# Gated feed-forward tiles: the rounded copies go from VectorE to ScalarE, one group later

## The reference, cut to what matters

```python
def conv_glu(h, w_up, conv_w, conv_b, w_down):
    seq = h.shape[1]
    up = h @ w_up
    up_pad = jnp.pad(up, ((0, 0), (CONV_WIDTH - 1, 0), (0, 0)))
    c = conv_b
    for j in range(CONV_WIDTH):
        c = c + conv_w[j] * up_pad[:, j:j + seq]
    gate, val = _split(c, (D_FF, D_FF))
    return (jax.nn.silu(gate) * val) @ w_down
```

## Time and profile before

| | us |
|---|---|
| median of 3 runs | 2054.72 |
| lowest, highest | 2047.13, 2056.26 |
| the profiled execution | 2048.42 |
| its span in the trace | 2046.5 |

### The profile page before, as it was taken

How to read it: one execution, slowest core, us unless ns; L and a number is a source line. 1 busy time by engine, 2 the same in 40 slices (tenths; PEclk the granted TensorE clock), 3 DMA queues, 4 the chain that set the end, 5 groups by cost and what they waited for, 6 DMA issues and landing times.

```text
span 2046.5 us, 44566 instructions
## 1 busy us (share of the span) xinstructions
PE 1883.6 (92%) x16390; PEld 1778.9 (87%) x16390; DVE 1293.0 (63%) x1943; ACT 1140.5 (56%) x1924; POOL 1037.9 (51%) x742
## 2 busy tenths in 40 slices
PE   8889889999999889888999999988899998879999
PEld 8778779999999778778999989866899997669999
DVE  3487725669913397824669963476786536777764
ACT  5653455456755654445557755665555457465544
POOL 5663449839986573448929985741200045411000
PEclk9999989999999999979999999997999999779999
DMA  6432015656665432005656664420366653205665
GB/s 208 122 103 71 23 39 158 176 145 186 188 187 164 124 114 74 23 22 154 176 151 179 187 173 133 150 89 21 112 183 202 193 166 113 72 17 154 186 193 173
DMA packets 146922, 271.20 MB, mean 133 GB/s; under 512 B 16433, under 2 KB 16946, under 8 KB 146738
## 3 DMA queue, kind: packets, MB, share of 16 engines
q1 hardware_dynamic: 145296, 264.97, 45.2%
q10 hardware_dynamic: 1442, 3.66, 0.5%
HBM read 267.52 MB, written 1.05 MB: 131 GB/s over the span
## 4 chain that ended last, share of the span: by engine, by line
PE 65%; DVE 15%; ACT 9%; POOL 8%; issue 3%; DMA 0%; ACTq 0%; DVEq 0%; SPq 0%
PE bank L649 63%; POOL ring_split L1317 8%; ACT arena L1351 7%; ACT hi_ring L1351 1%; PE bank L758 1%; DVE arena L1891 1%; DVE u L1961 1%; DVE arena L1890 1%; DVE arena L2062 1%; DVE arena L1975 1%; DVE arena L1974 0%; DVE arena L2109 0%; DVE arena L1973 0%; ACT L1351 0%; DVE arena L2464 0%
## 5 line engine op out<-in xcount | busy, mean ns | idle before, releaser
L1317 POOL TENSOR_TENSOR ring_split<-ring,hi_ring 128x512 fp32r<-128x512 f32 x682 | 969.1, 1449 | 736.7 <-ACT hi_ring L1351 730.9
L1351 ACT ACTIVATE hi_ring<-ring 128x512 fp32r<-128x512 f32 x1002 | 619.3, 630 | 555.1 <-PE bank L649 532.0
L649 PE MATMUL bank<-u_hi,hi_ring 128*128 128x256 f32 (+1 forms) x2480 | 676.1, 285 | 47.3 <-POOL ring_split L1317 39.7
L649 PE MATMUL bank<-u_split,hi_ring 128*128 128x256 f32 (+1 forms) x2480 | 665.4, 281 | 1.6 <-DVE u_split L1966 1.4
L649 PE MATMUL bank<-u_hi,ring_split 128*128 128x256 f32 (+1 forms) x2480 | 665.0, 281 | 0.0
L649 PEld LDWEIGHTS bank<-u_hi,hi_ring 128*128 128x128 f32 (+1 forms) x2480 | 452.3, 188 | 61.8 <-POOL ring_split L1317 41.1
L649 PEld LDWEIGHTS bank<-u_split,hi_ring 128*128 128x128 f32 (+1 forms) x2480 | 452.4, 188 | 4.0 <-DVE u_split L1966 2.4
L649 PEld LDWEIGHTS bank<-u_hi,ring_split 128*128 128x128 f32 (+1 forms) x2480 | 452.2, 188 | 0.9
L1999 DVE TENSOR_TENSOR ring_split<-ring,hi_ring 128x512 fp32r<-128x512 f32 x320 | 215.3, 694 | 111.9 <-ACT hi_ring L1351 108.1
L649 PE MATMUL bank<-arena 64*64 64x64 f32 (+6 forms) x3680 | 240.3, 255 | 14.6 <-DVE arena L2109 9.3
L649 PEld LDWEIGHTS bank<-arena 64*64 64x64 f32 (+3 forms) x3680 | 210.4, 155 | 49.5 <-issue 29.7
(11 more groups left out here) (246 smaller groups left out, 2407.0 us busy)
## 6 DMA issues: line engine op xcount, KB each, us to landing
ring<-in_stream SPq DMA_DIRECT2D x1002, 256.0 KB, 2.8
par<-in_params ACTq DMA_DIRECT2D x3, 637.0 KB, 4.3
h<-in_x SPq DMA_DIRECT2D x4, 256.0 KB, 4.3
cst<-in_cst SPq DMA_DIRECT2D x1, 993.0 KB
out<-h ACTq DMA_DIRECT2D x3, 256.0 KB, 2.8
par<-in_params ACTq DMA_DIRECT2D x1, 633.0 KB, 8.3
out<-h ACTq DMA_DIRECT2D x2, 128.0 KB, 2.3
msk<-in_masks SPq DMA_DIRECT2D x1, 104.0 KB
```

The lines of the kernel that those rows point to most:

```text
L649: ins = nc.tensor.matmul(o, l, r, start=start, stop=stop)
L1317: G.tensor_tensor(ring_lo[:, c, :], ring[:, c, :], hi_ring[:, q % HI_RING, :].bitcast(F32), ALU.subtract).then_inc(lo_by_pool, 1)
L1351: return nc.scalar.activation(o, i, f, **kw)
```

## The change

In the U loop of the first kind, VectorE no longer makes the rounded copy `hidden_hi`. ScalarE makes it, one turn later: in turn i it copies tile i - 2, behind its Silu of tile i - 1, once VectorE has signalled the product (new signal `hidden_in`). VectorE subtracts in the same turn, once ScalarE has signalled the copy (new signal `hidden_high`). Both loops have one turn more. ScalarE's wait before it reuses a `cb` buffer is now for the product instead of the low part. Three weight roundings that stood behind the table load now stand in the loop: one behind the last eviction, one ahead of the last Silu, one behind it.

```diff
@@ scalar, the U loop
-                for i in range(23):
+                for i in range(24):
                     if i < 22:
                         hi.upto(f"U{i}")
                         bank = B.wait(act, f"U{i}")
                         if i >= 4:
-                            act.wait_ge(S["hidden_ready"], past["hidden_ready"] + i - 3)
+                            act.wait_ge(S["hidden_in"], past["hidden_in"] + i - 3)
...
                         act.sem_inc(S["conv_in"], 1)
-                    if i:
+                    if i in (21, 22):
+                        hi.more()
+                    if 0 < i < 23:
                         act.wait_ge(S["conv_mid"], past["conv_mid"] + i)
                         C.link(A(cb[(i - 1) % 4][:, 0, :], cb[(i - 1) % 4][:, 0, :], ACT.Silu), S["conv_out"])
+                    if i == 22:
+                        hi.more()
+                    if i > 1:
+                        act.wait_ge(S["hidden_in"], past["hidden_in"] + i - 1)
+                        C.link(A(hidden_hi[:, i - 2, :], hidden[:, i - 2, :], ACT.Copy), S["hidden_high"])
                 nc.scalar.preload_act_table_set(LN_EXP)
@@ vector, the U loop
-                for i in range(23):
+                for i in range(24):
...
-                    if i:
+                    if 0 < i < 23:
                         dve.wait_ge(S["conv_out"], past["conv_out"] + i)
                         c_ = cb[(i - 1) % 4]
-                        C.link(V.tensor_tensor(hidden[:, i - 1, :], c_[:, 0, :], c_[:, 1, :], ALU.mult))
-                        split(C, hidden[:, i - 1, :], hidden_hi[:, i - 1, :], hidden_lo[:, i - 1, :], S["hidden_ready"])
+                        C.link(V.tensor_tensor(hidden[:, i - 1, :], c_[:, 0, :], c_[:, 1, :], ALU.mult), S["hidden_in"])
+                    if i > 1:
+                        dve.wait_ge(S["hidden_high"], past["hidden_high"] + i - 1)
+                        C.link(V.tensor_tensor(hidden_lo[:, i - 2, :], hidden[:, i - 2, :], hidden_hi[:, i - 2, :].bitcast(F32), ALU.subtract), S["hidden_ready"])
```

More of the change, by code:

```diff
@@ L410 @@
     "conv_in": (0, 22, 22, 20), "conv_mid": (0, 22, 22, 4), "conv_out": (0, 22, 22, 4),
-    "hidden_ready": (0, 22, 22, 16), "h_ready": (0, 10, 10, 10), "fresh_norm": (0, 1, 1, 0), "bi_ready": (0, 2, 2, 0),
+    "hidden_ready": (0, 22, 22, 16), "hidden_in": (0, 22, 22, 0), "hidden_high": (0, 22, 22, 0), "h_ready": (0, 10, 10, 10), "fresh_norm": (0, 1, 1, 0), "bi_ready": (0, 2, 2, 0),
     "bsg_ready": (0, 1, 1, 1), "gA_ready": (0, 2, 2, 0), "d_diff": (0, 0, 0, 1), "d_exp": (0, 8, 8, 4),
```

## The result

| | kernel before | changed kernel |
|---|---|---|
| median of 20 runs | 2051.3 us | 2060.5 us |
| lowest, highest | 2046.7, 2060.3 | 2051.4, 2068.5 |
| the profiled execution | 2048.4 | 2054.8 |
| its span | 2046.5 | 2053.1 |

The ratio is 1.004, with a 95% interval of 1.0026 to 1.0054: +8.2 us, between 5.3 and 11.1 (the two medians themselves lie 9.2 apart). The changed kernel is slower, by 0.3 to 0.5%.

What follows compares the result with a forecast made beforehand. TensorE, busy 92% of the span, was taken as the bound, the loop having 0.14 us slack. 11.6 - 1.4 - 1.2 = +9.0 us on 2054.7 gave 2063.7, predicted as 2063, range 2053 to 2070.

Steps and rivals of the forecast that it cites:

- The loop and its length: Up projection: eviction, Silu, copy, rounding, low part, matmul grows from 5.51 to 5.96 us; +11.6 us over two layers.
- The unhidden load: TensorE in the loop: a wait exposes a weight load, so matmul to eviction takes 1.71 us, not 1.61.
- The sign given for GpSimd: Steady up projection: GpSimd's idle time before its first low part grows from 0.16 to near 0.4 us.
- That 0.05: GpSimd: removing casts returns 0.05 us a group, in the third of four low parts, outside the loop, worth zero.
- Where the end's stall goes: End of up projection: TensorE's stall moves from the down projection's piece 4 to piece 7, 3.1 to 2.4 us.
- Rival B: Up projection: relieved GpSimd gets back 0.29 us per cast, groups don't grow; about 2053 us, chance 0.10.
- step (4): End of up projection: shorter stall gives -1.4 us over two layers, lowered clock gone -1.2; together -2.6 us.
- A: Rival: groups grow but the stage's end is repaired in full; +4.2 us, about 2059, chance 0.15.
- C: Rival: GpSimd's first low part takes 1.48 us, loop 6.14; +15.8 us, about 2070, chance 0.12 shared with D.
- D: Rival: ScalarE's copy stands idle for VectorE, each group losing more than in C; chance 0.12 shared with C.

Runs made afterwards that it cites:

- copy in another place: Changed kernel with ScalarE's tile copy moved one turn later, between the third and fourth weight roundings, except the last three tiles; ratio 1.0008.
- kernel before, once more: Kernel before, unchanged, traced a second time; again 5.65 us a group in U and a 3.0 us wait at the down projection.
- one more copy, 256 columns: Kernel before plus an unread 128x256 ScalarE copy behind the Silu in turns 2 to 21; 5.96 us a group.
- one more copy, 16 columns: Kernel before plus an unread 16-column ScalarE copy behind the Silu in turns 2 to 21; 5.765 us a group.
- moved roundings alone: Kernel before with only the three weight roundings moved, VectorE keeping its rounded copies; single run 2035.6 us, then ratio 1.0002 over twelve executions.
- copies alone: Changed kernel without the three moved roundings; single run 2065.6 us beside 2046.0 of the kernel before.
- last two products together: As copy in another place, with VectorE making its last two gate-and-value products back to back, ahead of three subtractions; ratio 0.9975 to the kernel before.
- two low parts by VectorE: As last two products together, with VectorE making low parts of the down projection's fifth and sixth pieces; ratio 0.9964, median 2041.0 us beside 2049.7.

## Why the prediction was right, point by point

**The loop and its length** were right to 0.01 us. Forecast: 5.96 a group, 0.22 for the first interval, +5.8 a layer. Measured: 5.965 a group, 5.96 for the first interval where it was 5.74, +5.9 and +5.8. The sum of four rows (2.44, 1.30, 0.06, 1.71) holds in the changed kernel term by term, the first of them longer by the copy's 0.45. The two extra copies show that the length of this loop sets the interval, whoever uses the copy, and the copy in another place shows that outside it the same copy costs nothing. The decisive step was not to divide ScalarE's work by its idle time. ScalarE was idle for 30% of the stretch, and 0.42 us of work went into it; but only 0.14 us of that idle time lay in the loop, the rest behind the roundings, where the copy costs nothing.

**The unhidden load** of 0.1 us was taken from a place where TensorE waited 1.9 us, and held where the piece's first matmul is only 0.12 late: 1.72 from the piece's first matmul to the eviction. In both places that matmul's row lasts 0.38 to 0.39 us instead of 0.28, and the next starts 0.22 behind it instead of 0.12. Without it the sum would have said 5.86. The sign given for GpSimd, an idle time of near 0.4 ahead of its first low part, was measured as 0.53: the group grew by 0.31, and its four low parts got 0.05 shorter. That 0.05 was forecast right in size and wrong in place: not the third low part became as short as one alone, but the fourth (1.48 to 1.30), while the third went from 1.34 to 1.48.

**Where the end's stall goes** was right. Forecast: pieces 4 to 6 in time, last product at 6.8 us after the eviction, TensorE at 10.7. Measured: 6.77 and 10.64. The forecast had no wait for a hidden tile ahead of it; the trace has one that costs 0.5, so the seventh piece costs 1.6 instead of about 2.3. On VectorE the price of GpSimd's work beside it is large: in the changed kernel's rows above a product takes 1.39 us and a subtraction 1.40 while a low part runs, and the next subtraction, with GpSimd idle, 0.42. On GpSimd it is small: from 470 to 550 us its mean low part went from 1402 to 1389 ns with the casts gone, 4 x 13 ns = 0.05 us a group, as read from the earlier trace rows. Rival B supposed that each removed cast hands GpSimd its full 0.29 us; no run shows that, and B did not come about.

**What the end gives** was mis-sized, in step (4). The forecast was -0.7 a layer for the wait and -1.2 once for the clock. The gaps in D's first 16 us fell by 0.4 and 0.6, a little less; the clock did stay up there in the second layer of the changed kernel. But D as a whole got 2.7 and 3.6 us shorter. In the first layer the rest, 2.3 us, is a term that the sum did not have: behind the waits the matmuls of D came 0.1133 us apart instead of 0.1178 (the mean from 580 to 620 us). In the changed kernel and in the kernel before, at the same granted clock:

```profile
578.00:618.00 40.00, 40.00 (x356) 40.00 (x355) 4.67 (x5) 20.22 (x33) 39.07 (x32) 1.00 0.68 194
```

```profile
580.00:620.00 40.00, 40.00 (x342) 40.00 (x341) 4.68 (x5) 19.80 (x32) 37.32 (x30) 1.00 0.65 185
```

I took 0.118 for a constant of TensorE. In the second layer the mean spacing of D is nearly the same in both traces, 0.1143 changed and 0.1145 before (steps under 0.15 us). There 1.2 us are the clock as forecast, and the remaining 1.8 lie behind a second wait that neither the change nor the forecast touches: in both kernels TensorE waits some 3 us for a low part, 42 to 44 us into this D. The kernel before then ran for a stretch at the lowered clock, the changed one did not. Before, then changed:

```profile
1232.20:1237.00 4.80, 4.80 (x28) 4.80 (x29) 0.00 (x0) 1.29 (x3) 4.80 (x4) 0.64 0.33 109
```

```profile
1232.00:1237.00 5.00, 4.95 (x43) 4.95 (x44) 0.00 (x0) 2.27 (x4) 5.00 (x5) 1.00 0.42 125
```

From U2's eviction to D's end the changed kernel therefore lost 3.3 and 2.2 us a layer in its trace, 5.4 in all, where the forecast had 9.0: the shorter spacing took off 2.3, the second clock 1.8, and the waits gave 0.4 less than forecast. The measured +8.2 (5.3 to 11.1) allows 5.4 and 9.0 alike, and so does not tell how much of these two terms came with the change and how much with that one execution. For the clock it was the execution in part: behind this second wait the twelve traces are split six to six.

**The number.** 2063 was made on the median of three runs, 2054.7; over twenty it is 2051.3. The difference, +9.0 against +8.2, was closer than the level. That it came within 1 us is in part luck, since terms of 2 us were missing from the sum and the interval is 6 us wide; what the runs support is +11.6 in U and a small gain at the end. Rivals A and C are excluded by the rows above: the seventh piece was late, and the first low part took 1.30. So is D: the 14 copies from 470 to 550 us had only 0.4 us of idle time ahead of them in all.

## What to carry to other kernels

Before work is moved to an engine with idle time, draw the loop that runs through it and add up the loop's length without waits; the difference from the bottleneck's time per turn is what the loop can take, however idle the engine is: here 5.65 - 5.51 = 0.14 us, with ScalarE idle for 30%. The same instruction three roundings further on, behind those that others wait for, cost nothing here: 5.653 us against 5.965 a group. At the end of a stage look at what the relieved engine runs beside, since with GpSimd newly busy VectorE's product and subtraction took 1.4 us instead of 0.43 and the stall only changed its cause.

## What the runs showed of the hardware

Both points come from the twelve traces of these kernels. Beside each trace stand, in us: the time from the first to the last matmul of D in the third and the fourth layer; the matmuls counted from 585 to 615 us, in D of the first layer, at a granted clock of 1.00; the longest step from one matmul's start to the next in D's first 16 us, first and second layer, and the longest in the middle of the second layer's D, each with the mean granted clock over the 3 us from the late matmul's start.

| trace | D, layers 3 and 4 | matmuls, 585 to 615 | layer 1: step, clock | layer 2: step, clock | middle of layer 2: step, clock |
|---|---|---|---|---|---|
| kernel before | 86.93, 86.93 | 257 | 3.14, 1.00 | 3.15, 0.52 | 3.14, 0.64 |
| kernel before, once more | 90.34, 90.33 | 257 | 3.14, 1.00 | 3.15, 1.00 | 3.12, 0.62 |
| changed kernel | 90.33, 90.33 | 267 | 1.74, 1.00 | 1.74, 1.00 | 2.95, 1.00 |
| one more copy, 256 columns | 90.33, 90.33 | 267 | 3.14, 0.50 | 3.14, 0.53 | 2.90, 0.60 |
| one more copy, 16 columns | 90.33, 90.33 | 267 | 3.07, 0.50 | 3.06, 0.58 | 2.95, 1.00 |
| moved roundings alone | 86.93, 90.34 | 267 | 3.60, 1.00 | 3.59, 0.50 | 2.92, 1.00 |
| moved roundings alone, timed | 90.33, 90.33 | 268 | 3.60, 0.76 | 3.59, 0.73 | 2.97, 1.00 |
| copies alone | 90.34, 90.33 | 267 | 4.61, 0.50 | 4.53, 0.50 | 2.97, 1.00 |
| copy in another place | 90.33, 90.33 | 267 | 1.74, 1.00 | 1.74, 1.00 | 2.97, 1.00 |
| last two products together | 90.34, 86.93 | 267 | 0.43, 1.00 | 0.70, 1.00 | 2.94, 0.53 |
| two low parts by VectorE | 86.93, 86.93 | 267 | 0.52, 1.00 | 0.80, 1.00 | 2.90, 0.52 |
| two low parts by VectorE, timed | 90.33, 90.33 | 267 | 0.52, 1.00 | 0.80, 1.00 | 2.97, 0.67 |

**Two spacings at one clock.** D of the second kind is 768 matmuls of 128x128 by 128x256 without a wait, at a granted clock of 1.00. It took 86.93 us six times and 90.33 or 90.34 eighteen times and nothing else, that is 0.1133 or 0.1178 us a matmul, and 3.4 us from one to the other. The same program had both in two executions, and the kernel with the last two products together and the one with the moved roundings alone had both in one. In D of the first layer both traces of the kernel before had 257 matmuls in 30 us. All ten traces of the other eight kernels had 267 or 268 there, also the kernel with one copy of 16 columns more, so in this stage the spacing seems to go with the program, and every edit tried moved it. What chooses is open. Two stages of 3.4 us can make up part of the 13.6 us by which the twenty executions of the kernel before spread (an estimate from the table), and a change of a few us should be read stage by stage.

**The lowered clock** behind a wait of 3 us comes and goes with the execution. In the second layer of the kernel before it stood in the first trace (0.51 over 3 us; the earlier trace rows) and not in the second, though the wait was the same 3.03 us. In the seven traces whose matmul at the start of D starts 3.06 to 4.61 us behind the one before, ten of the fourteen such waits were followed by it; in the other five traces, with steps of 0.43 to 1.74 us, it never stood there. Behind the step of 2.90 to 3.14 us in the middle of the second layer's D, which every kernel here has, it stood in six of twelve traces. In the first trace of the kernel before it cost 1.2 us behind the one wait and some 1.6 behind the other. So the traces bear out that a change which shortens the first wait also saves the clock, on average less than the 1.2 us that one trace showed for the kernel before: of its four first waits in two traces only one had it.
